# Sparse-attention decoder layer: the gate is multiplied into the exponentials, and each query row has one accumulation

## The chip, the core and the metric

The kernel computes one decoder layer on one core of a Trainium2 chip. The engines are TensorE (PE; its weight loads are listed as PEld), VectorE (DVE), ScalarE (ACT) and GpSimd (POOL), each with its own in-order instruction stream; SyncE (SP) issues DMAs. Streams are ordered against each other by semaphores alone. The metric is the device time in microseconds (us). Before the change the median of three runs is 1367.74 us (1365.91 to 1371.22).

## The reference, cut to what matters

The layer normalises `x`, projects it, runs two groups of heads (attention and a short convolution), adds the output projection, and ends with a gated feed-forward part. Only the attention is touched. For each of 8 query heads (two key/value groups of 4 heads) there are three branches, each a softmax of its own, and the three results are weighted by a gate per token, head and branch:

```python
s_c = einsum(qc, k_cmp) - slopes5 * d_c            # compressed keys, 63 of them
p_c = masked_softmax(s_c, d_c >= 0)
o_c = einsum(p_c, v_cmp)
...                                                # selected blocks: o_s, over all earlier keys
...                                                # window of 512 keys: o_w
return gc[..., 0:1] * o_c + gc[..., 1:2] * o_s + gc[..., 2:3] * o_w
```

With 1024 tokens there are 16 selection blocks of 64 keys, and 16 are selected, so the selected branch sees all earlier keys. Each softmax is exp(s - max) / denominator; gate and denominator are both one number per token, head and branch.

## The kernel before

Tokens are cut into 8 tiles of 128. A **query row** is one tile `i` of queries in one key/value group `g`, with its four heads: 16 rows. Its work stands in one **block** for `i` under 3 (all branches) and in two from there on, a block of the selected branch (S) and one of the window (W); the compressed branch (64 columns) rides in one of the two. That gives 26 blocks, numbered 0 to 25 in program order, 13 for each group. Block 22 is S of tile 6, 23 is W of tile 6, 24 is S of tile 7 and 25 is W of tile 7, all of the second group. S of tile `i` has `i`+1 key tiles of 128 columns for each head (8 at tile 7), W at most 5.

Two things are done for a block.

- Its four **units**, one for each head (`U`, 104 in all): PE writes scores to PSUM (`scores`, L1929, L1930 and the masks L1941), DVE takes the negated maximum (`row_max`, L1503), ACT writes the exponentials to SBUF and their sum to `den` (`exponentials`, L1119). The buffers of exponentials are `E` (two sets of four rows, by parity of the block) and `E_C` for the compressed branch.
- Its **steps**, one for each branch and key tile (148 in all): PE turns the 128x128 pieces of the four heads (`turn_step`, L1977), ACT copies them rounded to one operand (L1128), DVE subtracts to get the rest (L1538), PE multiplies both parts by the values (`values`, L1994 and L1995), two steps later, and accumulates in PSUM bank 7. A ring of three PSUM banks holds the turned pieces.

`steps_behind(U)` gives a quarter of the steps of the block one before `U`'s block, so that steps of block n stand behind the scores of block n+1, on every engine in the same order.

The steps of one block and branch are a **group**: 48 groups. After each, ACT copies the bank out (`copy_out`, L1135), PE turns the result back (`turn_out`, L2003, four transposes), DVE adds the two halves of the values' precision (`add_halves`, L1530), and POOL multiplies by gate over denominator (`weigh`, L880), which DVE had made in `coefficients(n)` (L1513 to L1518) at the second unit of the next block. POOL adds the three branches (L885, L888), and ACT squares the sum for the norm (L1140).

POOL's stream has beside these only the parts of the queries that `queries` makes (L838, L845) at six of the units. The next weights and the residual input are loaded by SP once all steps are done (`pv_done`).

Of the kernel before, what the change touches and what calls it, by code (L numbers as in the profile page):

```python
# [24 lines left out]
F32 = mybir.dt.float32  # L25
# [6 lines left out]
P = 128  # L32
# [12 lines left out]
CW = 64  # L45
# [98 lines left out]
STEPS, GROUPS, BLOCK_AT = [], [], []  # L144
for n_block, (g_block, i_block, kind_block) in enumerate(BLOCKS):
    BLOCK_AT.append(len(STEPS))
    for br_group, tiles_group in branches(i_block, kind_block):
        STEPS += [(n_block, br_group, j_tile, len(GROUPS)) for j_tile in tiles_group]
        GROUPS.append((n_block, br_group, len(STEPS) - len(tiles_group), len(STEPS) - 1))
BLOCK_AT.append(len(STEPS))  # L150
NS, NG = len(STEPS), len(GROUPS)
# [3 lines left out]
LAST_OF = {last: group for group, (_, _, _, last) in enumerate(GROUPS)}  # L155
ROW_OF = {group: ROWS[GROUPS[group][0]] for group in range(NG)
          if group + 1 == NG or ROWS[GROUPS[group + 1][0]] != ROWS[GROUPS[group][0]]}
# [13 lines left out]
KEYS_DONE = 34  # L171
def steps_behind(unit):

    n, h = divmod(unit, GROUP)
    if n == 0:
        return range(0)
    first, count = BLOCK_AT[n - 1], BLOCK_AT[n] - BLOCK_AT[n - 1]
    return range(first + count * h // GROUP, first + count * (h + 1) // GROUP)

# [11 lines left out]
def hybrid_layer(nc, xT, w_units, w_cmp1, w_cmp2, params_d, consts_d, masks_d, alibi_q, alibi_k, outT):  # L191
    with ExitStack() as ctx:  # L192
# [120 lines left out]
        E = [[F1[:, 11 + h, :] for h in range(GROUP)], [F1[:, 5 + h, :] for h in range(GROUP)]]  # L313
        E_C = nc.alloc_sbuf_tensor_at("EC", [P, 2, GROUP, CW], F32, offset=r1_at + 4 * at_r[0])
# [3 lines left out]
        OS = PBm[:, 0:6 * GROUP * DH].rearrange("p (e b n) -> p e b n", e=2, b=3)  # L318
        SQ_HEADS = PBm[:, 6 * GROUP * DH:7 * GROUP * DH].rearrange("p (a b) -> p a b", a=2)
# [6 lines left out]
        def e_cols(n, br, h, j):  # L326

            _, i, kind = BLOCKS[n]
            if br == CMP:
                return E_C[:, i % 2, h, :]  # L330
            at = j - max(0, i - WT) * (br == WIN) + (i + 1) * (br == WIN and kind == KEYS_OF_ALL)
            return E[n % 2][h][:, at * P:(at + 1) * P]
# [4 lines left out]
        def unit_parts(U):  # L337
# [3 lines left out]
            lead, e = CW * CMP_FIRST[i], E[n % 2][h]  # L341
            compressed = (CMP, 0 if lead else CMP_IN_B[i], CW, E_C[:, i % 2, h, :])
# [5 lines left out]
            return [(WIN, 0, window, e[:, 0:window])] + [compressed] * (not CMP_FIRST[i])  # L348

# [36 lines left out]
        o_step, o_ready, cmp_den = sem("o_step"), sem("o_ready"), sem("cmp_den")  # L386
# [400 lines left out]
        def _(pool):  # L787
# [82 lines left out]
            def weigh(group):  # L870

                n, br, _, _ = GROUPS[group]
                g, i, _ = BLOCKS[n]
                row = ROWS[n]
                order = [b for m, b, _, _ in GROUPS if ROWS[m] == row]
                part = lambda b: OS[:, i % 2, b, :]
                heads = lambda ap: ap.rearrange("p (h d) -> p h d", d=DH)
                pool.wait_ge(t_used, O_OF[group] + 1)
                pool.wait_ge(coef_ready, n + 1)
                nc.gpsimd.tensor_tensor(heads(part(br)), heads(part(br)),  # L880
                                        factor[:, i % 4, br * GROUP:(br + 1) * GROUP].rearrange("p (h o) -> p h o", o=1)
                                        .broadcast_to([P, GROUP, DH]), ALU.mult).then_inc(o_step, 1)
                if br == order[1]:
                    pool.wait_ge(o_step, 4 * row + 2)
                    nc.gpsimd.tensor_tensor(part(order[0]), part(order[0]), part(br), ALU.add).then_inc(o_step, 1)  # L885
                if br == order[2]:
                    pool.wait_ge(o_step, 4 * row + 4)
                    nc.gpsimd.tensor_tensor(F1[:, Q0 + 2 * g:Q0 + 2 * g + 2, i * P:(i + 1) * P],  # L888
                                            part(order[0]).rearrange("p (a b) -> p a b", a=2),
                                            part(br).rearrange("p (a b) -> p a b", a=2), ALU.add).then_inc(o_ready, 1)  # L890

            def behind(s):
                if s - TURN_LAG in LAST_OF:
                    weigh(LAST_OF[s - TURN_LAG])

            for U in range(NU + GROUP):
                if U in QUERIES_AT and QUERIES_AT[U][2] % 2 == 0:
                    queries(*QUERIES_AT[U])
                for s in steps_behind(U):
                    behind(s)  # L900
            for s in range(NS, END):
                behind(s)
# [92 lines left out]
        def _(act):  # L995
# [126 lines left out]
            def split_step(s):  # L1122
                n, br, j, group = STEPS[s]
# [6 lines left out]
            def copy_out(group):  # L1130

                act.wait_ge(pv_done, GROUPS[group][3] + 1)
                if group > 1:
                    act.wait_ge(tr_ready, O_OF[group - 2] + 1)
                nc.scalar.activation(OT[group % 2], PS[:, O_BANK, :], ACT.Copy).then_inc(ot_copied, 1)  # L1135
# [7 lines left out]
            def behind(s, unit):  # L1143
# [8 lines left out]
                group = LAST_OF.get(s - SQUARE_LAG)  # L1152
                if group in ROW_OF:
                    head_squares(ROW_OF[group])

            waiting = None
            for U in range(NU + GROUP):
# [173 lines left out]
        def _(dve):  # L1331
# [175 lines left out]
            def coefficients(n):  # L1507
# [4 lines left out]
                if CMP in [br for m, br, _, _ in GROUPS if m == n]:  # L1512
                    nc.vector.tensor_reduce(den[:, i % 2, CMP * GROUP:(CMP + 1) * GROUP], E_C[:, i % 2, :, :], AX.X, ALU.add)\  # L1513
# [8 lines left out]
            def add_halves(group):  # L1522

                n, br, _, _ = GROUPS[group]
                _, i, _ = BLOCKS[n]
                at = O_OF[group]
                dve.wait_ge(tr_ready, at + 1)
                if ROWS[n] > 1:
                    dve.wait_ge(o_ready, ROWS[n] - 1)
                nc.vector.tensor_reduce(OS[:, i % 2, br, :].rearrange("p (h d) -> p h d", d=DH),  # L1530
                                        PS[:, T_BANK + at % T_RING, :].rearrange("p (h e d) -> p h d e", e=2, d=DH), AX.X, ALU.add)\
                    .then_inc(t_used, 1)

            def split_step(s):
                n, br, j, group = STEPS[s]
# [13 lines left out]
            for U in range(NU + GROUP):  # L1549
# [11 lines left out]
                if U > GROUP and U % GROUP == 1:  # L1561
# [249 lines left out]
        def _(pe):  # L1811
# [155 lines left out]
            def turn_step(s):  # L1967

                n, br, j, group = STEPS[s]
                at, rows = T_OF[s], CW if br == CMP else P  # L1970
                pe.wait_ge(ex_ready, GROUP * (n + 1))
# [8 lines left out]
            def values(s):  # L1980

                n, br, j, group = STEPS[s]
                g, _, _ = BLOCKS[n]
                _, _, first, end = GROUPS[group]
                pe.wait_ge(t_used, T_OF[s] + 1)
                if s == first and group:
                    pe.wait_ge(ot_copied, group)
                elif s == first:
                    pe.wait_ge(vc_lo, KV)
                if s == first and ROWS[n] == TT:  # L1990
# [6 lines left out]
            def turn_out(group):  # L1997

                at = O_OF[group]
# [286 lines left out]
```

## Time and profile before

| | |
|---|---|
| median of the three runs | 1367.74 us |
| span of the profiled execution | 1366.2 us |
| busy PE, DVE, ACT, POOL | 94%, 68%, 44%, 36% of the span |
| first score of the attention | 289.6 us |
| first step of block 1 and of block 24 | 305.5 us, 561.1 us |
| last values of the attention | 583.8 us |
| squares of the last query row begin | 591.25 us |

The attention is about 302 us of the span. A time in the rows is counted from the start of the span. Matmuls overlap their neighbours, so PE's pace is read from the distance between the starts of two of them, not from the length of one.

### The profile page before, as it was taken

The numbers are of one execution on the slowest core, as the hardware profiler recorded it, in microseconds if no ns is written. First come the engines' busy times: TensorE is split into PE (matmuls) and PEld (weight loads), VectorE is DVE, ScalarE is ACT, GpSimd is POOL, SyncE is SP. The second block draws the span as 40 slices with busy tenths as digits, with TensorE's granted clock in tenths as the row PEclk, the third lists the DMA queues.
The fourth block names the chain that finished last, engine by engine and source line by source line (L and its number), as shares of the span: only waits on it lengthen the run. The fifth ranks groups of instructions, "written<-read, shape, count | busy, mean of one in ns | idle before, by whom it ended". The sixth has DMA issues, their size and how long they took to land. (4 is left out here: it accounts for less than half of the span.)

```text
span 1366.2 us, 17293 instructions
## 1 busy us (share of the span) xinstructions
PE 1289.5 (94%) x6234; PEld 1051.2 (77%) x6234; DVE 935.8 (68%) x1271; ACT 595.5 (44%) x1088; POOL 486.1 (36%) x380
## 2 busy tenths in 40 slices
PE   7999999988988899989997899999999999999996
PEld 6788888866777677768886688888888887888885
DVE  6444443169887888745358888888988887655665
ACT  6211121068777877733154333333333333644541
POOL 0776400033131321110045866766676653000211
PEclk9999999999999999999999999999999999999998
DMA  5677412000000000053201232323223326965653
GB/s 224 216 266 246 155 47 93 1 20 1 1 1 1 1 1 1 1 200 124 77 32 52 109 110 91 116 93 108 85 93 116 116 87 221 351 205 178 194 179 127
DMA packets 55934, 148.24 MB, mean 109 GB/s; under 512 B 5856, under 2 KB 6368, under 8 KB 54240
## 3 DMA queue, kind: packets, MB, share of 16 engines
q1 hardware_dynamic: 47776, 111.72, 23.8%
q0 software_dynamic: 8080, 35.50, 7.2%
q8 instruction: 47, 0.77, 0.2%
q14 instruction: 31, 0.25, 0.1%
HBM read 107.32 MB, written 40.11 MB: 108 GB/s over the span
## 5 line engine op out<-in xcount | busy, mean ns | idle before, releaser
L497 PE MATMUL PS<-R,wh 128*128 128x512 f32 x560 | 222.5, 397 | 14.4 <-DVE wl L489 14.4
L498 PE MATMUL PS<-R,wh 128*128 128x512 f32 x560 | 219.3, 392 | 0.0
L2112 PE MATMUL PS<-R,wh 128*128 128x512 f32 x480 | 188.7, 393 | 13.2 <-DVE wl L1624 8.4
L2113 PE MATMUL PS<-R,wh 128*128 128x512 f32 x480 | 187.5, 391 | 0.0
L2114 PE MATMUL PS<-R,wl 128*128 128x512 f32 x480 | 187.4, 390 | 0.0
L501 PE MATMUL PS<-R,wl 128*128 128x512 f32 x560 | 173.3, 391 | 0.0
L497 PEld LDWEIGHTS PS<-R,wh 128*128 128x128 f32 x560 | 106.1, 189 | 38.1 <-DVE wl L489 15.2
L498 PEld LDWEIGHTS PS<-R,wh 128*128 128x128 f32 x560 | 106.2, 190 | 22.4 <-issue 0.7
L501 PEld LDWEIGHTS PS<-R,wl 128*128 128x128 f32 x560 | 105.7, 189 | 22.3
L2126 PE MATMUL PS<-R,wh 128*128 128x512 f32 x308 | 120.6, 392 | 0.4 <-DVE R L1714 0.2
L2128 PE MATMUL PS<-R,wl 128*128 128x512 f32 x308 | 119.9, 389 | 0.0
L2127 PE MATMUL PS<-R,wh 128*128 128x512 f32 x308 | 119.8, 389 | 0.0
L2112 PEld LDWEIGHTS PS<-R,wh 128*128 128x128 f32 x480 | 90.6, 189 | 36.2 <-DVE wl L1624 16.5
L1235 ACT ACTIVATE wh<-F 128x512 fp32r<-128x512 f32 x110 | 67.6, 625 | 112.4 <-PE PS L2114 102.1
L1624 DVE TENSOR_TENSOR wl<-F,wh 128x512 fp32r<-128x512 f32 x110 | 108.6, 996 | 5.5 <-ACT wh L1235 5.5
L880 POOL TENSOR_TENSOR PBm<-PBm,factor 128x256 f32<-128x256 f32 x48 | 29.5, 614 | 225.4 <-DVE PBm L1530 225.4
L2114 PEld LDWEIGHTS PS<-R,wl 128*128 128x128 f32 x480 | 90.5, 189 | 19.1
L2113 PEld LDWEIGHTS PS<-R,wh 128*128 128x128 f32 x480 | 90.7, 189 | 18.7
L1503 DVE TENSOR_REDUCE nmax<-PS 128x1 f32<-128x64 f32 (+6 forms) x192 | 95.9, 538 | 4.0 <-PE PS L1941 3.3
L1119 ACT ACTIVATE F<-PS,nmax 128x640 f32<-128x640 f32 (+7 forms) x128 | 89.6, 705 | 12.4 <-DVE nmax L1503 12.2
L1709 DVE TENSOR_TENSOR wl<-raw,wh 128x512 fp32r<-128x512 f32 x77 | 59.0, 766 | 50.7 <-ACT wh L1276 50.4
L1538 DVE TENSOR_TENSOR ER<-PS,ER 128x512 fp32r<-128x512 f32 (+1 forms) x99 | 67.9, 686 | 29.3 <-ACT ER L1128 28.7
(232 smaller groups left out, 2685.0 us busy)
## 6 DMA issues: line engine op xcount, KB each, us to landing
raw<-in_w_units SPq DMA_DIRECT2D x55, 512.0 KB, 3.6
F<-gated SPq DMA_DIRECT2D x77, 256.0 KB, 4.0
W<-in_w_units POOLq DMA_DIRECT2D x11, 1024.0 KB, 7.8
weight_sums<-W POOLq DMA_DIRECT2D x11, 1024.0 KB, 4.9
raw<-weight_sums SPq DMA_DIRECT2D x44, 256.0 KB, 4.0
F<-in_w_units SPq DMA_DIRECT2D x20, 512.0 KB, 4.5
gated<-F SPq DMA_DIRECT2D x33, 256.0 KB, 2.1
raw<-in_w_units SPq DMA_DIRECT2D x33, 256.0 KB, 3.3
```

What stands on the lines that cost most here:

```text
L497: nc.tensor.matmul(out, w_h, hi(kt)[:, cols], start=first, stop=False)
L498: nc.tensor.matmul(out, w_h, lo(kt)[:, cols], start=False, stop=False)
L501: last = nc.tensor.matmul(out, w_l, hi(kt)[:, cols], start=False, stop=end)
L1119: last = nc.scalar.activation(e, pair(U % 2)[:, col:col + count], ACT.Exp, bias=nmax[:, br, i, h:h + 1], **total)
L1503: last = nc.vector.tensor_reduce(nmax[:, br, i, h:h + 1], pair(U % 2)[:, col:col + count], AX.X, ALU.max, negate=True)
L1624: nc.vector.tensor_tensor(product_slot(wl, n), block_of(m, PRODUCTS[q][0]), f32(product_slot(wh, n)), ALU.subtract)\
L2112: nc.tensor.matmul(out, w_h, operand(name, k, 0), start=fresh and k == 0, stop=False, skip_group_check=not fresh)
L2113: nc.tensor.matmul(out, w_h, operand(name, k, 1), start=False, stop=False, skip_group_check=not fresh)
L2114: last = nc.tensor.matmul(out, w_l, operand(name, k, 0), start=False, stop=k == 3, skip_group_check=not fresh)
L2126: nc.tensor.matmul(out, w_h, a_part(v, 0), start=fresh and k == 0, stop=False, skip_group_check=not fresh)
L2127: nc.tensor.matmul(out, w_h, a_part(v, 1), start=False, stop=False, skip_group_check=not fresh)
L2128: return nc.tensor.matmul(out, w_l, a_part(v, 0), start=False, stop=k == PAIRS - 1, skip_group_check=not fresh)
```

## The change

The gate over the denominator is no longer multiplied into the result of each group but into the exponentials, before they are turned. POOL's `weigh(n)` now waits for `coefficients(n)` and multiplies all exponentials of block n in place, one instruction for each head and branch (L914), and one for the four heads of the compressed branch (L909). `turn_step` waits for this (`es_ready`) and no longer for ACT. As all pieces now carry their weight, the three branches of a query row add up in PSUM: one accumulation, one copy, one turning back and one addition of halves for each of 16 rows, and the result goes straight to its place. POOL's additions are gone. Steps stand two blocks behind the scores (`BLOCK_LAG = 2`), and so the exponentials of three blocks are alive at a time; their places in a buffer of 10,240 columns come from a table (`E_STARTS`, checked by assertions). `E_C` has three places.

```diff
-STEPS, GROUPS, BLOCK_AT = [], [], []
+STEPS, BLOCK_AT = [], []
...
+ROW_STEPS = [[s for s, (n_block, _, _) in enumerate(STEPS) if ROWS[n_block] == row] for row in range(NROWS)]
+ROW_FIRST, ROW_LAST = [at[0] for at in ROW_STEPS], [at[-1] for at in ROW_STEPS]
...
+BLOCK_LAG = 2
+NU_END = NU + BLOCK_LAG * GROUP
 def steps_behind(unit):
-    n, h = divmod(unit, GROUP)
-    if n == 0:
+    n, h = divmod(unit - BLOCK_LAG * GROUP, GROUP)
+    if n < 0:
         return range(0)
-    first, count = BLOCK_AT[n - 1], BLOCK_AT[n] - BLOCK_AT[n - 1]
+    first, count = BLOCK_AT[n], BLOCK_AT[n + 1] - BLOCK_AT[n]
     return range(first + count * h // GROUP, first + count * (h + 1) // GROUP)
...
-        E = [[F1[:, 11 + h, :] for h in range(GROUP)], [F1[:, 5 + h, :] for h in range(GROUP)]]
+        E = F1[:, 5:15, :].rearrange("p a b -> p (a b)")
...
-            def weigh(group):
...
+            def weigh(n):
+                _, i, _ = BLOCKS[n]
                 pool.wait_ge(coef_ready, n + 1)
...
+                weights = lambda br, h, count=1: factor[:, i % 4, br * GROUP + h:br * GROUP + h + count]
+                if has_compressed(n):
+                    e = E_C[:, ROWS[n] % 3, :, :]
+                    nc.gpsimd.tensor_tensor(e, e, weights(CMP, 0, GROUP).rearrange("p (h o) -> p h o", o=1)
+                                            .broadcast_to([P, GROUP, CW]), ALU.mult)
+                for h in range(GROUP):
+                    for br, _, count, e in unit_parts(GROUP * n + h):
+                        if br != CMP:
+                            last = nc.gpsimd.tensor_tensor(e, e, weights(br, h).broadcast_to([P, count]), ALU.mult)
+                last.then_inc(es_ready, 1)
+
+            for U in range(NU_END):
                 if U in QUERIES_AT and QUERIES_AT[U][2] % 2 == 0:
                     queries(*QUERIES_AT[U])
...
+                if U % GROUP == 0 and 0 < U <= NU:
+                    weigh(U // GROUP - 1)
...
-            def copy_out(group):
-                act.wait_ge(pv_done, GROUPS[group][3] + 1)
...
+            def copy_out(row):
+                act.wait_ge(pv_done, ROW_LAST[row] + 1)
...
-                act.wait_ge(o_ready, row + 1)
+                act.wait_ge(t_used, O_OF[row] + 1)
                 nc.scalar.activation(SQ_HEADS, F1[:, Q0 + 2 * g:Q0 + 2 * g + 2, i * P:(i + 1) * P], ACT.Square,
...
-                if U > GROUP and U % GROUP == 1:
+                if U % GROUP == 1 and GROUP < U <= NU + 1:
                     coefficients(U // GROUP - 1)
...
-                pe.wait_ge(ex_ready, GROUP * (n + 1))
+                pe.wait_ge(es_ready, n + 1)
```

The first piece of order is POOL's, of before, at the end of the attention: the multiplications of a group's result, and the additions.

```order
L885 TENSOR_TENSOR PBm<-PBm 128x256
L880 TENSOR_TENSOR PBm<-PBm,factor 128x256
L888 TENSOR_TENSOR F<-PBm 128x2x128
L904 MEMSET F 128x1024
```

POOL's, of the changed kernel, for blocks 22 to 25 (`F` is the buffer of exponentials, `PBm` that of the compressed branch).

```order
L914 TENSOR_TENSOR F<-F,factor 128x896 x4
L914 TENSOR_TENSOR F<-F,factor 128x640 x4
L914 TENSOR_TENSOR F<-F,factor 128x1024 x4
L909 TENSOR_TENSOR PBm<-PBm,factor 128x256
L914 TENSOR_TENSOR F<-F,factor 128x640 x4
L923 MEMSET F 128x1024
```

Where a group cost an instruction of 256 columns, a block now costs four of up to 1024.

PE's, of before, one unit of block 24's scores (L1929 to L1941), and behind it a step of block 23.

```order
L1929 MATMUL PS<-wh,R 128x512
L1930 MATMUL PS<-wl,R 128x512
L1941 MATMUL PS<-masks 128x128
L1977 MATMUL PS<-consts,F 128x128 x4
L1994 MATMUL PS<-ER,R 128x512
L1995 MATMUL PS<-ER,R 128x512
```

PE's, of the changed kernel, the same unit's scores (now L1944 to L1956), and behind it two steps of block 22, with a turning back (L2018) of the row before them.

```order
L1944 MATMUL PS<-wh,R 128x512
L1945 MATMUL PS<-wl,R 128x512
L1956 MATMUL PS<-masks 128x128
L1992 MATMUL PS<-consts,F 128x128 x4
L2009 MATMUL PS<-ER,R 128x512
L2010 MATMUL PS<-ER,R 128x512
L2018 MATMUL PS<-consts,F 128x128 x4
L1992 MATMUL PS<-consts,F 128x128 x4
L2009 MATMUL PS<-R 128x512
L2010 MATMUL PS<-R 128x512
```

The heavy scores of an S block stood beside the few steps of a W block; now they stand beside the steps of the S block before, and the light W with W.

## Rows read from the trace of the kernel before

**Rows 1.** The page's busy times: us, share of the span, instructions.

```profile
PE 1289.5 (94%) x6234; PEld 1051.2 (77%) x6234; DVE 935.8 (68%) x1271; ACT 595.5 (44%) x1088; POOL 486.1 (36%) x380
```

**Rows 2.** Stretches of the attention: bounds, length, busy us by engine, granted clock, DMA.

```profile
289.60:305.50 15.90, 12.26 (x77) 10.02 (x77) 11.19 (x38) 11.93 (x47) 6.46 (x8) 0.79 0.11 22
305.50:561.00 255.50, 232.59 (x1519) 185.14 (x1519) 217.32 (x418) 201.38 (x490) 60.24 (x81) 0.99 0.00 1
561.00:591.70 30.70, 25.77 (x158) 20.38 (x157) 17.92 (x33) 15.88 (x37) 4.94 (x8) 1.00 0.21 80
```

**Rows 3.** Waits in the attention: who waited for whom, us, times, longest.

```profile
POOL PBm L880 <- DVE PBm L1530: 225.4, 43, 14.2
DVE ER L1538 <- ACT ER L1128: 28.7, 44, 1.7
PEld PS L1929 <- ACT F L1119: 17.1, 22, 2.5
```

**Rows 4.** Groups by line: shapes, count, busy us, mean ns, idle before.

```profile
L1530 DVE TENSOR_REDUCE PBm<-PS 128x256 f32<-128x512 f32 x48 | 32.6, 681 | 4.8 <-PE PS L2003 4.8
L2003 PE MATMUL PS<-consts,F 128*128 128x128 f32 x192 | 30.2, 282 | 2.0 <-DVE R L1538 1.0 <-DVE ER L1538 1.0
L1135 ACT ACTIVATE F<-PS 128x512 f32<-128x512 f32 x48 | 28.8, 599 | 2.4 <-PE PS L1995 2.3
```

**Rows 5.** Timeline of PE in a step: start us, us, engine, line.

```profile
568.17 0.48 PE L1994 MATMUL PS<-ER,R 128*128 128x512 f32 x1
568.48 0.39 PE L1995 MATMUL PS<-ER,R 128*128 128x512 f32 x1
568.71 0.60 PE L1977 MATMUL PS<-consts,F 128*128 128x128 f32 x4
569.07 0.48 PE L1994 MATMUL PS<-R 128*128 128x512 f32 x1
```

**Rows 6.** POOL's groups by line and shape, whole span.

```profile
L880 POOL TENSOR_TENSOR PBm<-PBm,factor 128x256 f32<-128x256 f32 x48 | 29.5, 614 | 225.4 <-DVE PBm L1530 225.4
L888 POOL TENSOR_TENSOR F<-PBm 128x256 f32<-128x256 f32 x16 | 11.7, 732 | 1.3
L806 POOL TENSOR_TENSOR W<-W 128x512 f32<-128x512 f32 x11 | 14.2, 1294 | 6.4 <-DMA W<-in_w_units 6.3
L789 POOL MEMSET F<- 128x1024 f32 x1 | 1.0, 957 | 33.4 <-PE PS L418 33.4
```

**Rows 7.** Timelines: first turns of blocks 0, 1, 22, 23, 24, 25; coefficients of 22, 24.

```profile
297.57 1.06 PE L1977 MATMUL PS<-consts,F 128*128 128x128 f32 x4
...
305.53 0.66 PE L1977 MATMUL PS<-consts,F 128*128 128x128 f32 x4 [0.85 <-ACT F L1119]
...
539.02 0.60 PE L1977 MATMUL PS<-consts,EC 128*64 128x128 f32 x4
...
544.28 0.17 DVE L1518 TENSOR_TENSOR factor<-inverse,gates 128x8 f32<-128x8 f32 x1
...
551.50 0.61 PE L1977 MATMUL PS<-consts,F 128*128 128x128 f32 x4
...
561.06 0.64 PE L1977 MATMUL PS<-consts,F 128*128 128x128 f32 x4
...
565.97 0.16 DVE L1518 TENSOR_TENSOR factor<-inverse,gates 128x4 f32<-128x4 f32 x1
...
573.43 0.66 PE L1977 MATMUL PS<-consts,F 128*128 128x128 f32 x4 [0.80 <-ACT EC L1119]
```

**Rows 8.** Two DVE lines: count, shortest/median/longest ns, first and last start us.

```profile
L1460 DVE SCALAR_TENSOR_TENSOR R<-F,R x16: 685/687/1627, 282.1 to 471.9; 64x512 fp32r<-64x512 f32 x16
...
L1624 DVE TENSOR_TENSOR wl<-raw,wh x30: 678/1176/2899, 739.8 to 1103.5; 128x512 fp32r<-128x512 f32 x30
```

**Rows 9.** Timeline of the attention's end: the last addition of halves, the last squares.

```profile
587.64 1.29 DVE L1530 TENSOR_REDUCE PBm<-PS 128x256 f32<-128x512 f32 x2 [4.81 <-PE PS L2003]
...
591.25 0.42 ACT L1140 ACTIVATE PBm<-F 128x256 f32<-128x256 f32 x1 [6.39 <-POOL F L888]
```

More of the change, by code:

```diff
@@ L154 @@
 END = NS + SQUARE_LAG
-LAST_OF = {last: group for group, (_, _, _, last) in enumerate(GROUPS)}
-ROW_OF = {group: ROWS[GROUPS[group][0]] for group in range(NG)
-          if group + 1 == NG or ROWS[GROUPS[group + 1][0]] != ROWS[GROUPS[group][0]]}
+LAST_OF = {last: row for row, last in enumerate(ROW_LAST)}
 VALUES_AT = (30, 33)
@@ L340, in unit_parts @@
             _, i, kind = BLOCKS[n]
-            lead, e = CW * CMP_FIRST[i], E[n % 2][h]
-            compressed = (CMP, 0 if lead else CMP_IN_B[i], CW, E_C[:, i % 2, h, :])
+            lead, e = CW * CMP_FIRST[i], E[:, E_STARTS[n][h]:E_STARTS[n][h] + widths(n)]
+            compressed = (CMP, 0 if lead else CMP_IN_B[i], CW, E_C[:, ROWS[n] % 3, h, :])
             own, window = P * (i + 1), P * min(i + 1, WT + 1)
@@ L1122, in split_step @@
             def split_step(s):
-                n, br, j, group = STEPS[s]
+                n, br, j = STEPS[s]
                 rows = slice(0, CW if br == CMP else P)
@@ L1151, in behind @@
                     later_values_hi(s)
-                group = LAST_OF.get(s - SQUARE_LAG)
-                if group in ROW_OF:
-                    head_squares(ROW_OF[group])
+                if s - SQUARE_LAG in LAST_OF:
+                    head_squares(LAST_OF[s - SQUARE_LAG])
             waiting = None
-            for U in range(NU + GROUP):
+            for U in range(NU_END):
                 if U in QUERIES_AT and QUERIES_AT[U][2] % 2:
@@ L1547, in behind @@
                     split_step(s)
-            for U in range(NU + GROUP):
+            for U in range(NU_END):
                 if U - PREP_LAG in QUERIES_AT:
@@ L1980, in values @@
             def values(s):
-                n, br, j, group = STEPS[s]
-                g, _, _ = BLOCKS[n]
-                _, _, first, end = GROUPS[group]
+                n, br, j = STEPS[s]
+                g, row = BLOCKS[n][0], ROWS[n]
+                first, end = ROW_FIRST[row], ROW_LAST[row]
                 pe.wait_ge(t_used, T_OF[s] + 1)
-                if s == first and group:
-                    pe.wait_ge(ot_copied, group)
+                if s == first and row:
+                    pe.wait_ge(ot_copied, row)
                 elif s == first:
                     pe.wait_ge(vc_lo, KV)
-                if s == first and ROWS[n] == TT:
+                if s == first and row == TT:
                     pe.wait_ge(t_used, V_OF[VALUES_AT[-1]] + 1)
@@ L1995, in values, with turn_out @@
                 nc.tensor.matmul(out, v, EL[s % ER_RING][rows, :], start=False, stop=s == end).then_inc(pv_done, 1)
-            def turn_out(group):
-                at = O_OF[group]
-                pe.wait_ge(ot_copied, group + 1)
+            def turn_out(row):
+                at = O_OF[row]
+                pe.wait_ge(ot_copied, row + 1)
                 pe.wait_ge(t_used, at - T_RING + 1)
                 for h in range(GROUP):
-                    last = nc.tensor.transpose(PS[:, T_BANK + at % T_RING, h * P:(h + 1) * P], OT[group % 2][:, h * P:(h + 1) * P], ident)
+                    last = nc.tensor.transpose(PS[:, T_BANK + at % T_RING, h * P:(h + 1) * P], OT[row % 2][:, h * P:(h + 1) * P], ident)
                 last.then_inc(tr_ready, 1)
@@ L2023, in behind @@
                     values(s - PV_LAG)
-            for U in range(NU + GROUP):
+            for U in range(NU_END):
                 if U < NU:
```

91 lines of the change are left out of this document (38 added, 53 removed).

## The prediction

> **What bounds the kernel now.** I read the page's busy times first: PE is busy 94% of the span [rows 1], so what saves only DVE's or ACT's time gives little unless PE waits for it. Then the stretches of the attention: PE is busy 232.6 of the 255.5 us between the first turn of block 1 and that of block 24, DVE 217.3, ACT 201.4, and POOL 60.2 [rows 2]. Three engines are within a sixth of each other and POOL is nearly free. The waits say the same: POOL sits 225.4 us waiting for DVE's additions of halves, DVE 28.7 us for ACT's rounded copies, PE 17.1 us for the exponentials that free a score bank [rows 3]. So the stage is a loop of three engines led by PE, and POOL is on it nowhere. The change puts POOL into it, between DVE's coefficients and PE's first turn of a block. The reader is to look not at POOL's sum but at one interval at a time: from PE's first turn of block n-1 to its first turn of block n.
>
> **What goes.** 32 of 48 groups lose their end. On PE that is four transposes each: a turn of four takes its place in PE's stream from 568.71 to 569.07, 0.36 us [rows 5], so 32 x 0.36 = 11.5 us. On DVE it is 32 x 0.68 = 21.8 us, on ACT 32 x 0.60 = 19.2 us [rows 4], and POOL loses about 54 us of its small operations (48 x 0.614, and 32 additions of 0.73 to 0.78) [rows 6]. If nothing else changed, PE's 11.5 us is the gain, for PE leads; the others' savings lie beside it.
>
> **What POOL gets.** All exponentials are multiplied: 67,584 columns in 128 instructions, and 16 instructions of 256 columns for the compressed branch. The nearest row of such an instruction is the old multiplication by a factor spread over columns, 614 ns for 256 [rows 6]. The trace has none of more columns. With two full inputs 256 columns take 732 ns and 512 take 1294, that is 2.20 ns a column and 0.17 us for the instruction [rows 6]. If the 0.17 us is also in the 614 ns, the spread factor costs 1.73 ns a column. I take this, as it is the same form of operand. It gives 128 x 0.17 + 67,584 x 1.73 ns + 16 x 0.61 = 21.8 + 116.9 + 9.8 = 148 us. The upper end is 2.20 ns a column with the rest of the 614 ns (0.05 us) for the instruction: 6.4 + 148.7 + 9.8 = 165 us. The lower end is POOL's fastest pace, a fill of 1024 columns in 957 ns [rows 6], 0.93 ns: 63 us and the rest, under 100. As a sum 148 us beside 255 would hide. As a delay within each block it doesn't.
>
> **An interval.** The first turn of block 24 was at 561.06 and its coefficients were done at 565.97 + 0.16 = 566.13: 5.1 us later. For block 22 it is 539.02 to 544.45, 5.4 us [rows 7]. After the change the same chain (scores, maximum and exponentials of the last units, coefficients) begins at PE's first turn of block n-1, with one step of W beside it in place of two of S. A step is 0.31 + 0.23 + 0.36 = 0.9 us of PE's stream [rows 5], so the chain is about 4.2 to 4.5 us. Then POOL needs for block 24 four times 0.17 + 1024 x 1.73 ns, 7.8 us; for block 22 four times 1.72 and 0.61, 7.5 us. With 0.1 us for the semaphore the intervals that end at the turns of 24 and 22 are 12.1 us. Before they were 561.06 - 551.50 = 9.6 us [rows 7] and as much for 22. PE has work for about 9 us in them, scores of W beside W's five steps: 4.5 us for the steps, and 1.2 us for a unit's scores, which is what the interval from block 24 to 25 leaves (573.43 - 561.06 - 8 x 0.9 = 5.2 us for four units and one turning back) [rows 7]. It waits out the rest, and with it all that stands behind the turn in its stream: the next scores, and so DVE's maxima and ACT's exponentials. Here the two lags work against the change. POOL's heavy blocks (S) have PE's light interval as their cover, and the light ones (W, 5.1 us) the heavy interval.
>
> **The sum.** I worked every interval so, from block 2 to block 24, with chain times like the two shown. In 13 POOL comes last (tile 2 and W of tile 3 in both groups, tile 1 in the second, and S of tiles 4 to 7 in both): 135 us before, 141.5 after, and 3.7 more because the interval before block 7 also carries the making of queries and won't shrink: 145. The other ten, mostly ending at a W block, stay PE's. They lose a group's end each but now have S's scores beside S's steps, where they took 551.50 - 539.02 = 12.5 us with W's scores [rows 7]; I take 117 for 120.5. So 262 for 255.5: +7 (rounded up, for POOL's place in the queue behind the queries' parts).
>
> **Start and end.** Steps begin one block later: 305.53 - 297.57 = 8.0 us [rows 7] with scores alone. At the end the scores of the last block (four units of 1.2 us) no longer stand beside the steps of block 24. The chain from the last addition of halves to the squares loses POOL's part: the second of the two additions ended at 588.93 and the squares began at 591.25 [rows 9], so 2.3 us go. 8.0 - 4.9 - 2.3, about +1; I count 0.
>
> **Two smaller prices.** DVE instructions with both inputs in SBUF are longer where POOL works: L1624 takes 678 ns at its shortest and 2899 at its longest, L1460 687 and 1627 in the attention [rows 8]. Some 18 such instructions (splits of queries and keys) fall among the steps; POOL is busy half of the time, so nine meet it, each delayed by about 0.9 us, half of a long POOL instruction; 8 us on DVE, a third of it on the way: +3 us. The Trainium skill (SBUF — State Buffer, Who interferes with whom) says that such an instruction and a GpSimd instruction that reads SBUF exclude each other for the whole instruction, and that one with a PSUM input doesn't contend; the pairs of row 8 agree with the first. The coefficients' product (L1518) is of this kind too but comes when POOL has finished the block before. Second, the granted clock was 0.79 in the first 16 us of the attention, where PE had least to do, and 0.99 in the long stretch [rows 2]; waits of 2 to 4 us a dozen times will bring some of the low level (1.2 GHz) back. I put 3 us.
>
> Together 7 + 0 + 3 + 3 = +13 us on the span of 1366.2. The profiled span stands 1.5 us under the median of the runs, so the time is 1366.2 + 13 + 1.5 = 1381 us. Nothing behind the attention changes: its loads wait for the last values, as before.
>
> **Rivals.**
>
> *POOL is slower, at its two-input pace.* At 2.20 ns and 0.05 us an instruction, S of tile 7 takes 9.2 us and not 7.8, and over the 13 intervals and those that tip over it is 11 us more: 1392. For it: every two-input row of POOL has this pace. Against it: 614 ns for 256 columns is already under their 732. The Trainium skill (GPSIMD Engine Reference, Elementwise — side-by-side cycle accounting) gives about 2.6 cycles an element for a two-input operation as the floor of its read port, and advises VectorE for elementwise work; by it all inputs count alike and this rival is the case. The two-input rows agree, the 614 ns row doesn't.
>
> *POOL keeps up.* If a factor that is one number for a whole row costs no reading, near the fill's 0.93 ns, S of tile 7 takes 4 x (0.17 + 0.95) = 4.5 us, the interval 4.2 + 4.5 = 8.7 is inside PE's 9, and what is left is the 11.5 us gain less 1 or 2: 1357. It decides below about 1.0 ns a column. For it: the spread factor was cheaper than a full input. Against: it was spread over 64 columns at a time and still cost 1.7.
>
> *It comes out even.* The three engines had 23 to 54 us of idle time in the long stretch [rows 2], and DVE and ACT lose 20 us each. If PE's waits for POOL let these catch up, and intervals that stay PE's shrink to PE's own work (107 us for 117, by 0.9 us a step and about 1.1 for a unit's scores over all blocks, an estimate from the same rows), the +7 is -3, and with cheap port and clock the time is 1367.
>
> *POOL's pace with more loss.* Both prices double and the pace is that of two inputs: 1402 and above.
>
> **Chances.** My forecast, POOL late at the old multiplication's pace, 1375 to 1388: 0.50. Two-input pace, 1388 to 1402: 0.20. Above: 0.06. Even, 1361 to 1375: 0.12. POOL keeps up, below 1361: 0.12. A measurement of this kernel tells 0.5% (6.8 us) from no change, so faster 0.12, same 0.12, slower 0.76. The range of 1363 to 1402 leaves some 0.1 below and 0.07 above.
>
> **What would show it.** In the changed profile L914 with 1024 columns at 1.9 us (2.3 by the first rival, 1.1 by the second), with 640 at 1.3; POOL busy about 150 us more than it loses. PE's wait for POOL at L1992, 25 to 35 us in a dozen pieces of 2 to 4 us, the longest before S of tiles 6 and 7. The first turns of blocks 22 and 24 12 us behind those before them. L2018 with 64 transposes, L1530's and L1135's successors with 16. A lower granted clock in the long stretch. The last squares about 13 us later than 591.25, and the same length from there to the end. I am wrong if PE hardly waits for POOL, or if the time moves behind the attention.

## The result, and the profile of the changed kernel

| | before | after |
|---|---|---|
| median of its runs, same chip, us | 1368.45 | 1392.13 (1390.85 to 1394.55) |
| ratio | 1 | 1.0179 [1.0161, 1.0197] |
| span of the profiled execution, us | 1366.2 | 1391.1 |
| first turn of block 1 / of block 24, us | 305.5 / 561.1 | 315.3 / 596.0 |
| last squares, and from there to the end, us | 591.3 / 774.9 | 617.6 / 773.5 |

The change costs 23.7 us. All of it is inside the attention: behind the last squares the kernel is as long as before. The page's busy times, which answer to [rows 1]:

```profile
PE 1292.0 (93%) x6106; PEld 1047.8 (75%) x6106; DVE 921.7 (66%) x1239; ACT 581.4 (42%) x1056; POOL 578.0 (42%) x444
```

DVE and ACT are each busy 14 us less, POOL 92 more, and PE 2.5 more although it has 128 instructions fewer. The stretches that answer to [rows 2] (start, up to block 1's first turn; blocks 1 to 24; the end):

```profile
305.50:315.30 9.80, 7.81 (x38) 5.96 (x37) 6.00 (x14) 6.61 (x19) 5.94 (x10) 0.73 0.00 1
315.30:596.00 280.70, 232.89 (x1404) 180.49 (x1404) 203.71 (x387) 187.49 (x457) 144.26 (x131) 0.93 0.00 1
596.00:617.90 21.90, 19.80 (x114) 15.27 (x115) 12.61 (x20) 10.06 (x19) 6.37 (x5) 1.00 0.15 54
```

The long stretch has grown by 25.2 us. PE is busy as long in it as before (232.9 for 232.6) with 115 instructions fewer, and its granted clock is 0.93 where it was 0.99: part of its busy time is at the 1.2 GHz level, where the same work takes longer. The stretch's growth shows as PE's idle time, 47.8 us for 22.9. The waits of the attention, which answer to [rows 3] (who waited for whom, us in all, times, longest):

```profile
POOL PBm L909 <- DVE factor L1536: 105.9, 16, 10.4
POOL F L914 <- DVE factor L1536: 46.9, 10, 8.2
DVE ER L1553 <- ACT ER L1147: 46.7, 48, 3.2
...
PEld PS L1992 <- POOL F L914: 28.5, 16, 3.5
...
PE PS L1992 <- POOL F L914: 24.0, 13, 3.3
```

POOL is idle for more than 150 us and still the one that PE waits for, 24 us in 13 pieces. DVE's own wait for ACT went from 28.7 to 46.7 us, and ACT's for PE's turns ahead of these copies from 25.5 to 35.3: the others wait behind PE. POOL's groups, which answer to [rows 6] (count, busy us, mean ns, idle before):

```profile
L914 POOL TENSOR_TENSOR F<-F,factor 128x640 f32<-128x640 f32 x40 | 49.4, 1265 | 24.3 <-DVE factor L1536 24.3
L914 POOL TENSOR_TENSOR F<-F,factor 128x512 f32<-128x512 f32 x16 | 16.1, 1038 | 7.4 <-DVE factor L1536 7.4
L914 POOL TENSOR_TENSOR F<-F,factor 128x1024 f32<-128x1024 f32 x8 | 14.9, 1894 | 15.3 <-DVE factor L1536 15.3
...
L909 POOL TENSOR_TENSOR PBm<-PBm,factor 128x256 f32<-128x256 f32 x16 | 10.7, 670 | 105.9 <-DVE factor L1536 105.9
...
L914 POOL TENSOR_TENSOR F<-F,factor 128x128 f32<-128x128 f32 x16 | 5.8, 397 | 0.0
```

From 128 to 1024 columns the time goes from 397 to 1894 ns: 1.67 ns a column and 0.18 us an instruction. Timelines of PE and of POOL around block 24 (start us, us; the bracket is idle time and its releaser) answer to [rows 7]:

```profile
583.83 0.64 PE L1992 MATMUL PS<-consts,F 128*128 128x128 f32 x4
...
595.96 0.66 PE L1992 MATMUL PS<-consts,F 128*128 128x128 f32 x4 [3.06 <-POOL F L914]
```

```profile
588.21 0.16 DVE L1536 TENSOR_TENSOR factor<-inverse,gates 128x4 f32<-128x4 f32 x1
588.45 1.89 POOL L914 TENSOR_TENSOR F<-F,factor 128x1024 f32<-128x1024 f32 x1 [7.05 <-DVE factor L1536]
...
594.01 1.89 POOL L914 TENSOR_TENSOR F<-F,factor 128x1024 f32<-128x1024 f32 x1
```

This is the changed kernel in small. The coefficients are done 4.5 us after the first turn of block 23, POOL needs 7.5 us for the four heads, and PE, which had work for 9, waits 3.1 us. POOL itself had nothing to do for 7 us before.

What a wait does to the clock is seen ahead of block 15 (stretches, as above, with the granted clock third from the end):

```profile
484.00:490.80 6.80, 6.80 (x43) 4.61 (x42) 6.50 (x13) 5.69 (x15) 3.60 (x5) 1.00 0.01 2
490.80:494.10 3.30, 0.10 (x2) 0.00 (x0) 1.41 (x3) 0.40 (x3) 3.28 (x5) 1.00 0.00 0
494.10:495.00 0.90, 0.86 (x6) 0.82 (x7) 0.00 (x0) 0.17 (x1) 0.00 (x0) 1.00 0.00 0
495.00:502.00 7.00, 7.00 (x27) 4.58 (x25) 3.14 (x7) 4.25 (x12) 3.98 (x4) 0.51 0.00 0
502.00:508.00 6.00, 6.00 (x47) 5.16 (x46) 4.13 (x8) 4.01 (x10) 0.05 (x1) 1.00 0.00 0
```

PE waits 3.2 us for POOL, starts at full speed, and is then at 1.2 GHz for 7 us, in which it gets 27 matmuls done where it does 47 in the next 6. Over the attention 54.5 us are at the low level, in eight pieces, against 13.7 in three before. The two longest pieces, 17 and 10 us, begin at the attention's start and in a wait of 4.1 us for ACT near 320 us. Five of the other six, 24 us together, begin in a wait of 2 us or more for POOL or within 2 us behind it. The level doesn't fall behind each such wait: at blocks 22 and 24 PE waits 2.9 and 3.1 us, and the clock stays at 1.00.

**The intervals.** The prediction argued by the interval from PE's first turn of one block to that of the next. They can be read off PE's timeline by counting turns (148 in the attention), here in one profiled execution of each kernel; where the low clock falls differs between kernels, so a difference of a microsecond or two in a sum is not to be read. "13" are those ending at the blocks where the prediction had POOL last, "10" the others up to block 23:

| us | before | after | lag only | short weighing | waits and start filled | two halves | halves, start filled |
|---|---|---|---|---|---|---|---|
| first turn of block 0 at | 297.6 | 307.0 | 306.3 | 306.3 | 305.4 | 308.2 | 307.3 |
| 13 intervals | 135.0 | 150.7 | 127.8 | 122.6 | 152.4 | 129.1 | 127.5 |
| 10 intervals | 120.5 | 130.0 | 130.9 | 126.5 | 121.3 | 126.3 | 123.9 |
| block 24 to last squares | 30.2 | 21.6 | 25.8 | 21.3 | 21.6 | 22.4 | 22.4 |

### The profile page after: what moved, and what is told of

It is laid out like the page before. It is cut to its first block and busy times, and to the rows that moved or that the text cites. A ratio compares the mean times of both kernels' runs of the same rounds, so it can differ in the third digit from the quotient of the medians.

```text
span 1391.1 us, 16851 instructions
## 1 busy us (share of the span) xinstructions
PE 1292.0 (93%) x6106; PEld 1047.8 (75%) x6106; DVE 921.7 (66%) x1239; ACT 581.4 (42%) x1056; POOL 578.0 (42%) x444
## 5 line engine op out<-in xcount | busy, mean ns | idle before, releaser
L914 POOL TENSOR_TENSOR F<-F,factor 128x640 f32<-128x640 f32 (+7 forms) x128 | 135.1, 1087 | 46.9 <-DVE factor L1536 46.9
L533 PEld LDWEIGHTS PS<-R,wl 128*128 128x128 f32 x560 | 105.5, 188 | 22.4
L2141 PE MATMUL PS<-R,wh 128*128 128x512 f32 x308 | 120.5, 391 | 1.3 <-DVE R L1729 1.3
L1521 DVE TENSOR_REDUCE nmax<-PS 128x1 f32<-128x64 f32 (+6 forms) x192 | 95.8, 537 | 11.2 <-PE PS L1956 10.8
L1992 PE MATMUL PS<-consts,F 128*128 128x128 f32 x528 | 86.3, 289 | 16.6 <-POOL F L914 12.9
L1553 DVE TENSOR_TENSOR ER<-PS,ER 128x512 fp32r<-128x512 f32 (+1 forms) x99 | 67.9, 687 | 47.8 <-ACT ER L1147 46.7
L1138 ACT ACTIVATE F<-PS,nmax 128x640 f32<-128x640 f32 (+7 forms) x128 | 89.2, 701 | 22.9 <-DVE nmax L1521 22.6
```

The lines of the kernel that those rows point to most:

```text
L533: last = nc.tensor.matmul(out, w_l, hi(kt)[:, cols], start=False, stop=end)
L914: last = nc.gpsimd.tensor_tensor(e, e, weights(br, h).broadcast_to([P, count]), ALU.mult)
L1521: last = nc.vector.tensor_reduce(nmax[:, br, i, h:h + 1], pair(U % 2)[:, col:col + count], AX.X, ALU.max, negate=True)
L2141: nc.tensor.matmul(out, w_h, a_part(v, 0), start=fresh and k == 0, stop=False, skip_group_check=not fresh)
```

## The experiments

Theory A is the prediction's: POOL's time between coefficients and turn, block by block, is the loss. Theory B: the loss is the second block of lag. Theory C: it is TensorE's clock. Ratios are to the kernel before on the same chip.

**Short weighing.** POOL waits, signals and issues as in the changed kernel, but each of L914's instructions multiplies 8 columns only. The kernel leaves out the rest of the weighing: the other exponentials go on unweighted.

```diff
-last = nc.gpsimd.tensor_tensor(e, e, weights(br, h).broadcast_to([P, count]), ALU.mult)
+last = nc.gpsimd.tensor_tensor(e[:, 0:8], e[:, 0:8], weights(br, h).broadcast_to([P, 8]), ALU.mult)
```

> The changed kernel, in which each of POOL's multiplications of selected and window exponentials covers only 8 columns (the rest of the exponentials goes on unweighted: part of the computation is left out); the number of instructions and all waits are kept. Theory A (the loss is POOL's time between coefficients and first turn, with what it does to the clock): PE's wait for POOL at L1992 falls from 24 us to under 2, time 1355 to 1362, faster than before the change. Theory B (the loss is the second block of lag: heavy scores beside heavy steps, and 8 us of scores alone at the start): time stays over 1385. Theory C (half and half): about 1375.

Measured: 1359.84 us, 0.9945 [0.9929, 0.9962]. PE has no wait for POOL any more. POOL's time is 32.3 us of the changed kernel, more than its whole loss, and the rest of the change gains 8 us. In the table it is the 13 intervals that fall, by 28, and the others by 3: the blocks that the prediction named. Two of the waits that PE still has in it:

```profile
PE PS L1944 <- ACT F L1138: 13.6, 18, 1.8
...
PE PS L2009 <- ACT F L1154: 9.3, 8, 2.9
```

The first is a unit's scores waiting for the exponentials of a unit before (8.9 us in the kernel before, 18.0 in the changed one). The second is the first product of a row's values, into the one output bank, waiting until ACT has copied the row before out of it. PE's timeline at the longest of these waits:

```profile
356.38 0.50 PE L2009 MATMUL PS<-R 63*128 63x512 f32 x1
356.72 0.40 PE L2010 MATMUL PS<-R 63*128 63x512 f32 x1
357.05 0.66 PE L1992 MATMUL PS<-consts,F 128*128 128x128 f32 x4
360.62 0.76 PE L2009 MATMUL PS<-ER,R 63*128 63x512 f32 x1 [2.92 <-ACT F L1154]
361.18 0.62 PE L2010 MATMUL PS<-ER,R 63*128 63x512 f32 x1
```

The same two products take 0.50 and 0.40 us before the wait and 0.76 and 0.62 behind it: the low level comes behind this wait too. Ahead of the copy (L1154, at 359.89) ACT had exponentials of 768 columns (0.89 us) and a part of the keys (L1068, 0.62), and before them it had waited 2.3 us for a maximum that stood in DVE's stream behind parts of the keys (L1464, L1465).

**Lag only.** The kernel before with BLOCK_LAG 2, the buffers of the changed one and a third place for the compressed branch; the 48 groups, their endings and the weighing of results stay.

```diff
+BLOCK_LAG = 2
-    n, h = divmod(unit, GROUP)
+    n, h = divmod(unit - BLOCK_LAG * GROUP, GROUP)
-    first, count = BLOCK_AT[n - 1], BLOCK_AT[n] - BLOCK_AT[n - 1]
+    first, count = BLOCK_AT[n], BLOCK_AT[n + 1] - BLOCK_AT[n]
```

> The kernel before with steps two blocks behind the scores and the same buffers for exponentials as the changed one, but 48 groups, each ended and multiplied as before. Theory A: the lag alone costs little, 1368 to 1374 (8 us more at the start, 5 us back at the end, some us of lower clock). Theory B: 1385 or more.

Measured: 1376.84 us, 1.0077 [1.0057, 1.0097]: between what the two theories gave. The lag costs 9 us by itself. The 13 intervals shrink by 7.2 us and the other ten grow by 10.3; start and end together add 3.8. Three of the ten make up more than the growth, those ending at blocks 6, 10 and 13: 35.2 us before, 46.1 here. In the first two the steps of a long block now stand beside the scores of a long one, and all three have other units' keys or queries with them than before. The second seems to matter more: with the lag alone the intervals ending at blocks 6, 8 and 10 grow from 37.7 to 43.8, and those ending at 19, 21 and 23, the same pairs of blocks in the second group, where no keys and queries are made any more, from 34.8 to 36.8. The waits of this kernel's values line (L2027), behind those of before (L1994):

```profile
PE PS L1994 <- ACT F L1135: 10.8, 15, 1.6
PEld PS L1994 <- issue: 10.3, 20, 1.3
```

```profile
PEld PS L2027 <- issue: 17.2, 25, 3.9
...
PE PS L2027 <- ACT F L1168: 13.5, 15, 3.7
```

The longest wait for the copy out of the output bank went from 1.6 to 3.7 us. It is in the interval ending at block 13, and what stands ahead of the copy in ACT's queue is two parts of queries (L1090, L1092):

```profile
448.19 0.63 ACT L1090 ACTIVATE R<-F 64x512 fp32r<-64x512 f32 x1
...
448.85 0.63 ACT L1092 ACTIVATE R<-F 64x512 fp32r<-64x512 f32 x1
...
449.86 0.58 ACT L1168 ACTIVATE F<-PS 128x512 f32<-128x512 f32 x1
...
450.58 0.76 PE L2027 MATMUL PS<-R,VT 128*128 128x512 f32 x1 [3.65 <-ACT F L1168]
```

The waits for this copy account for some 3 us; the other part of the 10.3 was not taken apart. No run moved the keys, so that they are what makes these intervals long is argued from the two groups and the timelines, not shown.

**Waits and start filled.** Matmuls whose result is never read stand ahead of the first turns of eleven blocks, in the step's own bank and ahead of the wait for POOL, and four each behind the scores of units 3 to 7. **Waits filled only** is without the latter.

```diff
+FILL = {2: 7, 5: 5, 7: 3, 9: 11, 11: 8, 15: 10, 18: 4, 20: 6, 22: 9, 24: 10, 25: 3}
+FILL_START = {3: 4, 4: 4, 5: 4, 6: 4, 7: 4}
-                pe.wait_ge(es_ready, n + 1)
+                for k in range(FILL.get(n, 0) if s == BLOCK_AT[n] else 0):
+                    nc.tensor.matmul(PS[:, T_BANK + at % T_RING, :], masks[:, M_ID:M_ID + P], masks[:, 0:BANK], ...)
+                pe.wait_ge(es_ready, n + 1)
```

> The changed kernel with matmuls that nobody reads in the places where PE waits: 4 of 512 columns behind the scores of units 3 to 7, and 3 to 11 just ahead of the first turn of each of the 11 blocks for which PE waited for POOL, sized to end before POOL does. If the lower clock is a cause beside the waits: granted clock in 310 to 561 us rises from 0.92 to 0.97 or more, the waits stay, and the time falls by 5 to 10 us to 1382 to 1387. If the clock costs nothing (PE only runs slower where it would wait anyway): 1391 to 1394.

Measured: 1384.29 us, 1.0119 [1.0102, 1.0136].

> The changed kernel with the filling matmuls only ahead of the 11 first turns that wait for POOL, and none at the start. The filled kernel took 7.8 us less than the changed one. If the low clock that follows each wait is what these 7.8 us were: 1385 to 1387, with the start's 17 us at the low level as in the changed kernel. If it was the filling at the start: 1391 to 1393.

Measured: 1388.01 us, 1.0145 [1.0130, 1.0160], a microsecond above the range given. The stretches 289 to 310 and 310 to 561, first with both fillings, then with the waits' alone:

```profile
289.00:310.00 21.00, 17.65 (x116) 12.83 (x118) 14.59 (x47) 14.23 (x55) 9.27 (x18) 0.92 0.07 17
310.00:561.00 251.00, 219.51 (x1327) 164.58 (x1335) 187.32 (x361) 172.90 (x427) 133.69 (x129) 0.95 0.00 1
```

```profile
289.00:310.00 21.00, 16.41 (x86) 13.47 (x86) 13.67 (x44) 13.88 (x54) 8.36 (x17) 0.61 0.07 17
310.00:561.00 251.00, 219.31 (x1334) 165.95 (x1334) 186.92 (x360) 172.15 (x425) 132.46 (x129) 0.95 0.00 1
```

In the changed kernel the granted clock from 310 to 561 us is 0.92; it rises to 0.95 only, less than the 0.97 expected. With both fillings half of the low clock is gone (27.3 us are left of 54.5) for 7.8 us of time; the filled waits alone give 4.1. The 13 intervals don't shrink (152.4), so POOL decides them whatever the clock; the other ten fall from 130.0 to 121.3 (to 122.5 with the waits' filling alone), those ending at blocks 3 and 16 from 13.5 to 10.8 each. So a wait for POOL that the low level follows is paid twice: once itself, and once in the slower PE of the interval behind it. Theory C holds for a sixth to a third of the loss, not for its core.

**Two halves.** Coefficients and weighing in two parts, heads 0 and 1 as soon as their exponentials are there, heads 2 and 3 after theirs, in 18 of the 26 blocks. POOL's time stays, but in these blocks half of it moves ahead.

```diff
-                if U % GROUP == 1 and GROUP < U <= NU + 1:
-                    coefficients(U // GROUP - 1)
+                for part in PART_AT.get(U, []):
+                    coefficients(part)
-                for h in range(GROUP):
+                for h in range(h0, h1):
```

> The changed kernel with coefficients and POOL's multiplications in two halves for 18 of the 26 blocks (heads 0 and 1 two units earlier, then heads 2 and 3). POOL's work grows by 9 us and DVE's by about 12. Theory A: POOL has only half a block left when the last coefficients come, 3.9 us for S of tile 7 in place of 7.6, PE's wait for POOL falls from 24 us to under 5, time 1364 to 1372. Theory B: no help, 1392 to 1400 (DVE's added work).

Measured: 1369.25 us, 1.0012 [1.0003, 1.0022]. PE's waits at the turns for POOL:

```profile
PEld PS L2009 <- POOL F L926: 2.2, 2, 1.2
...
PE PS L2009 <- POOL F L926: 0.8, 1, 0.8
```

0.8 us for 24.0, with POOL as busy in the attention as in the changed kernel (149.0 us at these products for 145.8). 22.9 us of the loss are gone with an edit that takes nothing away (it adds 50 short instructions on DVE and 14 on POOL). It is mostly the place of POOL's time in the block that costs, not its amount. The kernel with short weighing is another 9.4 us faster; what these are was not taken apart, but 4.2 of them stand in the first turn of block 1 (317.8 us here, 313.6 there).

**Queries earlier**, in the changed kernel and with the halves: POOL makes its part of two queries ahead of the weighing in whose queue they stood.

```diff
+POOL_QUERIES_AT = {{9: 8, 42: 40}.get(U, U): q for U, q in QUERIES_AT.items() if q[2] % 2 == 0}
```

> The changed kernel with two of POOL's six makings of query parts put ahead of the multiplication they stood behind (unit 9 to 8, unit 42 to 40). In the changed kernel DVE waited 3.7 and 3.9 us for them (L1478). If these waits were on the way: 5 to 8 us less, 1384 to 1387. If PE would have waited there for POOL's multiplications anyway (these now start 3 us later): 1390 to 1393.

> Two halves and the earlier makings of queries together. In the two-halves kernel DVE no longer waited for POOL's query parts (0.4 us in all), so little is left for the shift: 1365 to 1370. If the queue of POOL still costs there: 1362.

Measured: 1390.63 us, 1.0174 [1.0154, 1.0195], and 1367.54 us, 1.0006 [0.9995, 1.0017]. Alone it is within the interval of no difference from the changed kernel; with the halves it is 1.7 us, which their intervals don't tell apart. Both lie in the range expected if the shift does little. It was tried for the one interval that is far off in the changed kernel, that ending at block 2 (17.8 us for 12.3). The timeline of all engines there:

```profile
315.22 1.48 POOL L877 TENSOR_SCALAR R<-F 64x512 fp32r<-64x512 f32 x1
...
316.73 1.09 DVE L1478 SCALAR_TENSOR_TENSOR R<-F,R 64x512 fp32r<-64x512 f32 x1 [3.73 <-POOL R L877]
...
319.04 0.31 ACT L1138 ACTIVATE PBm<-PS,nmax 128x64 f32<-128x64 f32 x1 [3.90 <-DVE nmax L1521]
...
320.53 0.79 PE L1944 MATMUL PS<-R 128*128 128x512 f32 x1 [4.12 <-ACT F L1138]
```

POOL makes the query only after weighing block 1; DVE waits 3.7 us for it with the next maximum queued behind, so ACT waits 3.9 and PE 4.1. With the queries earlier the interval is 13.6 for 17.8, yet the time hardly falls: PE's waits for POOL stay at 23.9 us. With halves the interval is 13.2, with this edit and the start filled too 11.9.

**Halves, start filled**, and **lag only, start filled**: the filling behind units 3 to 7 added to each.

> The same with 4 matmuls that nobody reads behind the scores of units 3 to 7, to hold the clock at the start. In the two-halves kernel PE ran at the low level for 17.1 us from 294.9. Theory C (the clock at the start is part of what the second block of lag costs): 4 to 6 us less than without the filling, 1360 to 1364, and faster than before the change. If PE's pace at the start doesn't decide (ACT and DVE do): no difference.

> The kernel before with two blocks of lag (1376.8) and the same filling at the start. Theory C: the lag's 9 us are the low clock of the start for the most part: 1369 to 1372. Otherwise, if the 9 us come from heavy scores beside heavy steps: 1375 to 1378.

Measured: 1365.20 us, 0.9978 [0.9968, 0.9988], and 1376.11 us, 1.0064 [1.0044, 1.0083]. The first is 2.3 us faster than without the filling, half of the 4 to 6 expected of the clock, and beats both kernels, if by 2.4 us only. The second shows that the lag's 9 us are not the clock at the start: filled, it gives back 0.7.

**Two heads on ACT.** In the same 18 blocks ACT multiplies heads 2 and 3 (a copy with a scale), POOL heads 0 and 1; with the earlier queries and the start filled.

```diff
+                            last = nc.scalar.activation(e, e, ACT.Copy, scale=factor[:, i % 4, br * GROUP + h:br * GROUP + h + 1])
```

> The changed kernel in which ACT, not POOL, multiplies the exponentials of heads 2 and 3 in the 18 blocks that the two-halves kernel splits (ACT's work grows by some 25 us, POOL's falls by 48, DVE's stays), with the query parts earlier and the start filled. Theory A: as the delay between coefficients and first turn is halved as well, and DVE is spared the halves' 10 us: 1360 to 1366, at least as fast as the halves with the same filling (1365.2). If ACT's added work stands before exponentials that PE's scores wait for: 1368 to 1375.

Measured: 1376.93 us, 1.0071 [1.0057, 1.0086], above both ranges given. PE's direct wait for POOL is 0.8 us (4.5 of the weight loads), but ACT is busy 198.7 us of the 251 from 310 to 561, where it had 184.3 in the version with halves and start filled:

```profile
310.00:561.00 251.00, 213.24 (x1305) 163.44 (x1304) 189.75 (x366) 198.67 (x474) 91.70 (x86) 0.96 0.00 1
```

```profile
310.00:561.00 251.00, 220.94 (x1392) 171.42 (x1390) 209.36 (x426) 184.25 (x452) 144.75 (x146) 0.97 0.00 1
```

The first row is this kernel, the second the halves' with the start filled; PE gets through 87 instructions fewer in the same stretch. PE's waits for ACT's exponentials and copies out are 28.3 us here and 22.0 there. POOL's slower time was the cheaper one once it came early enough: ACT is in the loop.

## Why the prediction was right, and where it was not

The sign, the mechanism and the wide range of 1363 to 1402 held; 1392.1 is 11 us above the forecast of 1381 and outside the 1375 to 1388 that had the chance of 0.50. It is also the figure of the first rival, POOL at its two-input pace, but that isn't what happened: the pace was the forecast's, and that the time falls on the rival's figure is chance. The 11 us have another source, the ten intervals below.

- *What goes.* 11.5 us of PE. On the others the lines lost what was said: the additions of halves take 10.9 us for 32.6, the copies out 9.5 for 28.8. DVE's busy sum falls by less, 14 us, in part for the price of the port below; why ACT's falls by 14 only was not looked into. From lag only to short weighing, the same step with everything else of the change, the medians fall by 17.0. 4.5 of it is the chain from block 24 to the squares, for which the prediction had 2.3 in another term. Right, if some 3 us low.
- *POOL's price.* 1.73 ns a column and 0.17 us predicted, 1.67 and 0.18 measured; 148 us in all, and it was 135.1 + 10.7 = 145.8. Right. By the Trainium skill (GPSIMD Engine Reference, Elementwise — side-by-side cycle accounting) a two-input operation has a floor of about 2.6 cycles an element. At the 1.2 GHz that it reckons with this is an estimate of 2.17 ns, and the rows of two full inputs agree, with 2.20 ns a column [rows 6]. The 1.67 ns a column of the spread factor are below it, so its floor doesn't hold for this operand.
- *An interval.* 12.1 us for those ending at blocks 22 and 24; measured 12.2 and 12.1. Right.
- *Thirteen intervals, 145 us.* 150.7. The one ending at block 2 alone grew by 5.5, from 12.3 to 17.8. The prediction counted POOL's place behind the queries as POOL being late for PE; what weighed there was the reverse, the query late for DVE behind the weighing.
- *The other ten, "I take 117 for 120.5".* **This is the step that failed.** They took 130.0, and two things are in the 13 us. The first is the low clock behind POOL's waits: with the waits filled the ten take 122.5, with the start filled too 121.3. The prediction had it outside this term, at 3 us for all of the attention. The second is the lag. The prediction took a long block's scores beside a long block's steps at the cost of the old pairing less a group's end, and it gave what is made at fixed units no price here. The three intervals ending at blocks 6, 10 and 13 were 35.2 together and are 42.5; they are 43.4 with the waits filled, 45.8 with short weighing and 46.1 with the lag alone, so it isn't POOL that makes them long. Where no keys and queries are made the term was nearly right: the intervals ending at 19, 21 and 23 took 34.8 before and 35.3 in the changed kernel, 33.9 with the waits filled. Light beside light, where the time should come back, is mostly among the thirteen that POOL decides. The lag by itself costs 9 us, and outside the start and the end the prediction gave it no price, since no instruction is added by it.
- *Start and end, 0.* First turn of block 1 9.8 us later, 8.6 us less from block 24 to the squares: +1.2. Right.
- *Port, 3 us.* It was reckoned as 8 us on DVE, a third of it on the way; the lines of keys and queries (L1478, L1465) take 20.0 us of DVE in the attention for 16.5. Of L1478, 12 of its instructions among the steps have a longest of 1560 ns, against 1090 with short weighing:

```profile
L1478 DVE SCALAR_TENSOR_TENSOR R<-F,R x12: 685/690/1560, 297.4 to 484.9; 64x512 fp32r<-64x512 f32 x12
```

```profile
L1478 DVE SCALAR_TENSOR_TENSOR R<-F,R x12: 684/686/1090, 296.7 to 468.2; 64x512 fp32r<-64x512 f32 x12
```

  (shortest, median, longest ns; changed kernel, then short weighing). The median doesn't move, so most meet no long POOL instruction. By the Trainium skill (SBUF — State Buffer, Who interferes with whom) a DVE instruction with two SBUF inputs contends with a GpSimd instruction that reads SBUF, and the pair of ports that they share is an exclusive lock; the 1560 ns agree with that. The mechanism is there, and the size small; how much of it reaches the end no run isolated.
- *Clock, 3 us.* 4.1 (waits filled), 7.8 with the start; the low level went from 13.7 to 54.5 us. But 41.0 us of low level are also in the kernel with short weighing, so it isn't POOL's waits alone that bring it: there it also follows waits such as the 2.9 us for ACT's copy.
- *What would show it.* PE's wait 25 to 35 us in a dozen pieces of 2 to 4 us: 24.0 in 13 (28.5 in 16 of the weight loads), seven of them over 2 us. S of tiles 6 and 7 in the two groups have 3.3, 2.5, 2.9 and 3.1 us, but tile 2 of the second group, block 15, has 3.2 too. L2018 with 64 transposes, L1545 with 16 reductions, as said:

```profile
L1545 DVE TENSOR_REDUCE F<-PS 128x256 f32<-128x512 f32 x16 | 10.9, 682 | 4.2 <-PE PS L2018 4.2
...
L2018 PE MATMUL PS<-consts,F 128*128 128x128 f32 x64 | 10.7, 294 | 0.0
```

  The squares were to be 13 us later and are 26, which is the whole miss in one number; from there on nothing changed, as said.

The sum over spans: 280.7 for the 268 predicted between blocks 1 and 24 (262 and the two small prices), +1.2 for 0 at the ends, -1.4 behind: 12.5; the span is 11.9 above its forecast, the rest is rounding (6.5 had been taken as 7). The 12.7 in the middle are 13.0 of the ten intervals and 5.7 of the thirteen, less the 6 set aside for port and clock.

The rival "it comes out even" rested on waits letting the others catch up. The ten intervals that stay PE's took 130.0 and not 107, those behind a wait at the low level longer still (13.5 us for 10.8 at blocks 3 and 16), and even with the waits and the start filled they take 121.3.

Open: how much of the 3 to 6 us by which the intervals ending at blocks 6 and 13 are longer with the lag alone is due to the keys and queries. The units at which these are made were left where the lag of one had them, and only two of POOL's parts were ever moved.

## What to carry to other kernels

An engine with idle time isn't free for work that stands between a producer and a consumer. Price it per block, as the time from its input to the consumer's next need, and if it is late, split its input so that it starts earlier: here that gave back 23 of 24 us without taking an instruction away. A deeper lag has a price of its own: pair the stages of every block anew and add up the longer ones, with what is bound to fixed places in the order, which now falls beside other blocks. And a wait of a few microseconds on TensorE can cost again in what follows, at the lower clock: here five of seven waits of 2 us or more did.

## What the runs showed of the hardware

- A product by a spread factor on POOL: 397, 856, 1265 and 1894 ns for 128, 384, 640 and 1024 columns in the changed kernel; 8 columns take 199, the median (short weighing).
- The same on ACT, a copy with a scale, 1024 columns:

```profile
L1165 ACT ACTIVATE F<-F,factor 128x1024 f32<-128x1024 f32 x4 | 4.4, 1152 | 0.0
```

- Unread matmuls in PE's waits gave 4.1 us in eleven waits and 3.7 more at the start of the attention. At the start alone they gave 2.3 us with the halves and 0.7 with the lag only.
- The low level followed five of the seven waits of 2 us or more for POOL (granted clock 0.51 behind the 3.2 us ahead of block 15), and none of the last two, 2.9 and 3.1 us.
